# Four gated branch products: the gates' read-back issued after the recurrence, products in place, the last branch summed block by block

## The chip, the cores and the metric

The kernel runs on one core of a Trainium2 chip. The metric is the device time of one launch in microseconds (us). The core has five engines that run their own instruction streams and meet at semaphores: TensorE (PE; its weight loads are PEld), VectorE (DVE), ScalarE (ACT), GpSimd (POOL) and SyncE (SP, which here only issues weight loads). A transfer is issued on a queue of SP or of POOL (SPq, POOLq) and lands later.

## The reference

The program is two layers of a "first block", followed by one "second block". In each layer of the first block a normed input `h` (256 tokens, width 1024) is projected; four mixers of width 256 (sparse attention, retention, the RWKV-7 recurrence, a short convolution) give one output each, and the branches are merged with gates, which are part of the same projection:

```
gate_m  = sigmoid(h @ w_in[:, gate columns of branch m])     m = 0..3, each 256 x 1024
merged  = sum over m of gate_m * (o_m @ w_branch[m])
x       = x + rms_norm(merged @ w_mix_out) * gain
```

The kernel writes sigmoid(z) as (tanh(z/2) + 1) / 2: the tanh is what is stored, a product is `(stored + 1) * (o_m @ w_branch[m])`, and the factor 1/2 is applied once when the sum is copied out. Cross attention with the memory `mem` and a feed-forward part follow, then the second block with its 32 experts.

## The kernel before, in words

Everything is kept transposed: channels on the 128 partitions, 256 tokens along a row. Matrix products are made from halves: each 1 MB unit of weights that SP loads into one of four ring slots is copied to a rounded high half by ScalarE (`upper`, a 128x2048 ACTIVATE of 1.9 us) and subtracted to a low half by VectorE (`lower_part`, a 128x2048 TENSOR_TENSOR of 2.3 us); TensorE then makes three matmuls for each product (`mm3`, line 583). The halves lie in three buffers. Each engine's program calls `unit()` once for each weight unit in the same order, and each call on ScalarE and VectorE splits as far as two units ahead (LOOK = 2). So the place of the `unit()` calls in each program sets where the splits stand in its queue. Call the four units of `w_branch` m0 to m3, and the first ones of `w_mix_out` m4 and m5: the call for m0 splits m2, and so on. SP may load into a slot when VectorE has made the low half of the unit that was in it (line 2710).

`fill_list` (line 142) names 27 projections of `h` that are strewn between the small dependent steps of the mixers, so that TensorE has work. The last 16 are the gates: for gate n, ScalarE writes the tanh into one of two staging buffers `stg` (line 1374), and GpSimd stores it to DRAM, `gate_d`, 256 KB each (`gates`, lines 2622 to 2629), because the on-chip memory is full of the recurrence's matrices. Gates 14 and 15 are made after `y_of(1)`, the recurrence's last step on TensorE (lines 890 to 894); between and behind them stand the mean and the variance of y (`ymean`, `yvar`), and there `mix end` is marked.

VectorE norms y (lines 2222 to 2235): subtract the mean, square (`ysq`), wait for ScalarE's root (`yvar`, line 1521), reciprocal, two products, scale and add, and gives the third branch's output `yout`; ScalarE copies its high half `oT2`, VectorE writes the low half.

GpSimd then waits for `mix end` on three engines and for all gate stores, and issues four read-backs of 1 MB into `L.Gt`, each 128 partitions by 2048 (lines 2662 to 2668), and the load of `mem` (line 2669). `L.Gt`, two buffers `L.mg` and `L.mt` of 2048 columns, and `L.mem` share the arena with the mixers' tiles.

TensorE makes the branch products in the order BRANCHES = (0, 1, 3, 2), four groups of 12 matmuls for each branch, each group into a PSUM bank (lines 900 to 910). There are eight banks in turn, so group 9 waits for VectorE to have emptied the bank of group 1. VectorE's loop (lines 2239 to 2250) makes, for each branch, `unit()`, a wait for that branch's read-back, and four products, each of 128x512 and each waiting for the one before (the wait in `stt`, line 1880): branch 0 into `mg`, the others into `mt`. GpSimd adds `mt` to `mg` for branches 1 and 3 (lines 2670 to 2675), slice by slice; for branches 3 and 2 the product waits until `mt`'s slice was added. VectorE adds the last branch itself, four slices in a row (lines 2251 to 2254), ScalarE copies each slice's high half into `hTv[0]` (`merged`, line 1532), and VectorE writes the four low halves (lines 2255 to 2258). With the last of them `tok_out` starts on TensorE (lines 911, 912).

The functions concerned, `pool`, `scalar` and `vector`, are called once for each engine:

Of the kernel before, what the change touches and what calls it, by code (L numbers as in the profile page):

```python
# [262 lines left out]
def build(nc, W, CW, CS, CO, PR, PR2, GB, x_in, mem_in, out, scratch, bias_d, gate_d):  # L263
    ctx = ExitStack()
    with ctx:
# [1003 lines left out]
        def scalar(ac, branch):  # L1269
# [70 lines left out]
            for l in range(2):  # L1340
# [178 lines left out]
                fill()  # L1519
                ac.wait_ge(s_dve, V["ysq", l])  # L1520
# [6 lines left out]
                for m in range(4):  # L1527
                    unit()
                for jj in range(4):
                    js = slice(2 * jj, 2 * jj + 2)  # L1530
                    ac.wait_ge(s_dve, V["sum", jj, l])
                    act(hTv[0][:, js, :], L.mg[:, js, :], ACT.Copy, "merged", jj, l, scale=0.5)
# [334 lines left out]
        def vector(ve, branch):  # L1867
# [99 lines left out]
            for l in range(2):  # L1967
# [257 lines left out]
                tt(L.t2, L.t1, L.t1, MUL, "ysq", l)  # L2225
                ve.wait_ge(s_act, A["yvar", l])
# [5 lines left out]
                tt(L.t1, L.t1, L.gg, MUL, "yout", l)  # L2232
                ve.wait_ge(s_act, A["oT2", l])
                lower(oT[2], L.t1, "oT", 2, l)
                V.mark("mix end", l)
                ve.wait_ge(s_pe, P["mix end", l])


                for n, m in enumerate(BRANCHES):
                    unit()  # L2240
                    ve.wait_ge(s_gin[m], 16 * (l + 1))
                    for jj in range(4):
                        gsl = L.Gt[:, 8 * m + 2 * jj:8 * m + 2 * jj + 2, :]
                        js = slice(2 * jj, 2 * jj + 2)
                        dst = L.mt if m else L.mg
                        ve.wait_ge(s_pe, P["merge", m, jj, l])
                        if n >= 2:
                            ve.wait_ge(s_pool, G["sum", BRANCHES[n - 1], jj, l])
                        stt(dst[:, js, :], gsl, 1.0, half(banks["merge", m, jj, l]), ADD, MUL, "merge", m, jj, l)
                        gone("merge", m, jj, l)  # L2250
                for jj in range(4):
                    js = slice(2 * jj, 2 * jj + 2)
                    ve.wait_ge(s_pool, G["sum", BRANCHES[2], jj, l])
                    tt(L.mg[:, js, :], L.mg[:, js, :], L.mt[:, js, :], ADD, "sum", jj, l)
                for jj in range(4):
                    js = slice(2 * jj, 2 * jj + 2)
                    ve.wait_ge(s_act, A["merged", jj, l])
                    stt(hTv[1][:, js, :], L.mg[:, js, :], 0.5, hTv[0][:, js, :].bitcast(F32), MUL, SUB, "merged", l)
# [355 lines left out]
        def pool(gp, branch):  # L2614
# [7 lines left out]
            def gates(l):  # L2622
                for n in range(16):
# [5 lines left out]
                    gp.dma_start(gate_d[:, 512 * g:512 * g + 512], flat(layers[l].stg[n % 2])).then_inc(s_gate[n % 2], 16)  # L2629

# [9 lines left out]
            for l in range(2):  # L2640
# [20 lines left out]
                gates(l)  # L2661
# [3 lines left out]
                for i in range(2):  # L2665
                    gp.wait_ge(s_gate[i], 16 * 8 * (l + 1))
                for m in range(4):
                    gp.dma_start(flat(L.Gt[:, 8 * m:8 * m + 8, :]), gate_d[:, 2048 * m:2048 * m + 2048]).then_inc(s_gin[m], 16)
                gp.dma_start(L.mem, mem_in.rearrange("b (t p) d -> p (b t) d", t=2)).then_inc(s_mem, 16)
                for m in BRANCHES[1:3]:  # L2670
                    for jj in range(4):
# [3 lines left out]
                        gp.tensor_tensor(L.mg[:, js, :], L.mg[:, js, :], L.mt[:, js, :], ADD).then_inc(s_pool, G("sum", m, jj, l))  # L2675
# [248 lines left out]
```

## Time and profile before

| | us |
|---|---|
| median of 3 runs (lowest to highest) | 2218.91 (2217.14 to 2219.31) |
| the profiled execution's own time | 2216.08 |
| its span in the trace | 2214.3 |
| TensorE busy | 1954.1 (88%) |
| VectorE busy | 1441.0 (65%) |
| ScalarE busy | 1145.8 (52%) |
| GpSimd busy | 70.0 (3%) |

In the trace, lines such as L202 or L212 are those of the small helpers of `Seq` (188 matmul, 198 activation, 202 tensor_tensor, 209 tensor_scalar with two operations, 212 scalar_tensor_tensor, 225 reciprocal, 231 dma_start), so the tiles and the time tell which step it is. "arena" and "rounded" are the working memory, "ring" the loaded weights, "hl" their halves, "ax" the mixers' outputs, "ht" the split input of the next product. A bracket at the end of a timeline line is the engine's idle time before it and who ended it. All microseconds inside the trace count from the span's start.

### The profile page before, as it was taken

Reading aid. Unit: us, or ns where it says so; the run is one execution under the profiler, and the core shown is the slowest. Engines: PE = TensorE matmul, PEld = TensorE weight load, DVE = VectorE, ACT = ScalarE, POOL = GpSimd, SP = SyncE. Lnnn points to the kernel's source line nnn. Section 1 sums busy time; section 2 is a strip of 40 time slices with the busy share of each in tenths; the row PEclk is TensorE's granted clock in tenths of the full one; section 3 lists DMA queues with packets and bytes.
Section 4 is the critical chain, followed back from the end, with each engine's and each line's share of the span. In section 5 each row is a group of like instructions: output and inputs, shape, how many; then the busy total and the mean of one; then the engine's idle time right before and its main releaser. Section 6 shows DMA issues by size and latency. Waiting matters only on the chain.

```text
span 2214.3 us, 30326 instructions
## 1 busy us (share of the span) xinstructions
PE 1954.1 (88%) x13010; PEld 1784.8 (81%) x13010; DVE 1441.0 (65%) x1379; ACT 1145.8 (52%) x1194; POOL 70.0 (3%) x94
## 2 busy tenths in 40 slices
PE   4988996897999788999699799797759999999997
PEld 3978996887998778998688798697657888888885
DVE  3677646535555567745643655665659989999996
ACT  2533333444444443233443444455349888888884
POOL 0000003000000000002100000000000000000000
PEclk9999998998999889999899999998869999999999
DMA  6333345433555333346443445331329989999994
GB/s 257 125 123 115 120 167 218 163 134 115 190 184 179 129 133 114 125 143 232 148 154 126 162 182 192 141 137 70 121 106 357 369 354 365 365 374 376 360 364 179
DMA packets 64523, 440.86 MB, mean 199 GB/s; under 512 B 7372, under 2 KB 7372, under 8 KB 14592
## 3 DMA queue, kind: packets, MB, share of 16 engines
q1 hardware_dynamic: 55296, 399.63, 48.2%
q0 software_dynamic: 8096, 35.30, 4.2%
q10 hardware_dynamic: 992, 3.93, 0.4%
q8 instruction: 104, 1.70, 0.3%
q14 instruction: 35, 0.29, 0.0%
HBM read 428.61 MB, written 10.23 MB: 198 GB/s over the span
## 4 chain that ended last, share of the span: by engine, by line
PE 67%; DVE 18%; ACT 10%; DMA 2%; issue 2%; POOL 1%; DVEq 0%; ACTq 0%; POOLq 0%
PE psum L188 65%; ACT hl L198 4%; DVE ring_low L202 3%; DVE arena L212 3%; DVE ht L202 2%; PE psum L192 2%; DVE hl L202 2%; DVE rounded L212 2%; DVE rounded L202 2%; DVE arena L202 2%; ACT arena L198 2%; POOL arena L202 1%; ACT gn L198 1%; ACT rounded L198 1%; DVE arena L225 1%
## 5 line engine op out<-in xcount | busy, mean ns | idle before, releaser
L202 DVE TENSOR_TENSOR hl<-ring,hl 128x2048 fp32r<-128x2048 f32 (+1 forms) x190 | 430.7, 2268 | 386.7 <-ACT hl L198 386.6
L188 PE MATMUL psum<-ht,hl 128*128 128x256 f32 x4992 | 625.8, 287 | 15.4 <-DVE hl L202 9.8
L198 ACT ACTIVATE hl<-ring 128x2048 fp32r<-128x2048 f32 (+1 forms) x286 | 536.3, 1895 | 193.0 <-PE psum L188 167.4
L188 PEld LDWEIGHTS psum<-ht,hl 128*128 128x128 f32 x4992 | 611.6, 194 | 26.2 <-DVE hl L202 10.3
L198 ACT ACTIVATE arena<-psum 128x512 f32<-128x512 f32 (+7 forms) x242 | 123.4, 510 | 498.4 <-PE psum L188 475.3
L188 PE MATMUL psum<-hl,ax 128*128 128x512 f32 (+1 forms) x1608 | 356.1, 358 | 6.1 <-DVE ax L202 5.0
L188 PEld LDWEIGHTS psum<-hl,ax 128*128 128x128 f32 x1608 | 267.9, 194 | 47.4 <-DVE ax L202 5.3
L202 DVE TENSOR_TENSOR ring_low<-ring,hl 128x2048 fp32r<-128x2048 f32 x96 | 215.3, 2285 | 21.6 <-ACT hl L198 21.6
L188 PE MATMUL psum<-arena 128*128 128x128 f32 (+6 forms) x1520 | 198.7, 300 | 33.7 <-ACT arena L198 23.6
L188 PEld LDWEIGHTS psum<-arena 128*128 128x128 f32 (+2 forms) x1520 | 181.8, 185 | 46.3 <-ACT arena L198 25.3
L188 PE MATMUL psum<-hl,ht 128*128 128x256 f32 (+1 forms) x1056 | 132.9, 288 | 30.3 <-DVE ht L212 27.5
L188 PEld LDWEIGHTS psum<-hl,ht 128*128 128x128 f32 x1056 | 130.6, 197 | 32.5 <-DVE ht L212 27.9
L188 PE MATMUL psum<-rounded 128*128 128x512 f32 (+1 forms) x576 | 123.6, 352 | 9.2 <-DVE rounded L202 3.6
L192 PE MATMUL psum<-cst,arena 128*128 128x128 f32 x286 | 51.1, 347 | 88.4 <-DVE arena L212 64.4
L202 DVE TENSOR_TENSOR arena<-arena 128x512 f32<-128x512 f32 (+8 forms) x148 | 90.3, 610 | 59.1 <-ACT arena L198 43.0
L192 PEld LDWEIGHTS psum<-cst,arena 128*128 128x128 f32 x286 | 44.2, 182 | 94.9 <-DVE arena L212 42.0
L202 DVE TENSOR_TENSOR rounded<-arena,hl 128x2048 fp32r<-128x2048 f32 x48 | 107.7, 2285 | 18.2 <-ACT hl L198 18.2
L188 PE MATMUL psum<-ax,hl 128*128 128x256 f32 x768 | 102.5, 299 | 14.9 <-DVE arena L212 14.9
L188 PEld LDWEIGHTS psum<-ax,hl 128*128 128x128 f32 x768 | 100.7, 207 | 16.6 <-DVE arena L212 15.6
L188 PEld LDWEIGHTS psum<-rounded 128*128 128x128 f32 x576 | 93.6, 196 | 23.9 <-issue 3.7
L202 DVE TENSOR_TENSOR ht<-ht_raw,hl 128x2048 fp32r<-128x2048 f32 x46 | 103.2, 2285 | 3.8 <-ACT hl L198 3.8
L188 PE MATMUL psum<-hl,rounded 128*128 128x512 f32 x256 | 104.1, 406 | 0.0
(116 smaller groups left out, 2026.8 us busy)
## 6 DMA issues: line engine op xcount, KB each, us to landing
ring<-W SPq DMA_DIRECT2D x284, 1024.0 KB, 5.0
arena<-W SPq DMA_DIRECT2D x48, 1024.0 KB, 7.9
ht_raw<-W SPq DMA_DIRECT2D x46, 1024.0 KB, 7.4
gate_d<-arena POOLq DMA_DIRECT2D x32, 256.0 KB, 3.8
arena<-gate_d POOLq DMA_DIRECT2D x8, 1024.0 KB, 9.8
gn<-GB POOLq DMA_DIRECT2D x10, 512.0 KB, 4.0
arena<-GB POOLq DMA_DIRECT2D x6, 512.0 KB, 5.1
ring<-W SPq DMA_DIRECT2D x4, 512.0 KB, 3.2
```

The source lines that it names most:

```text
L188: return Nothing() if self.e is None else self.e.matmul(o, a, b, start=start, stop=stop, skip_group_check=skip_group_check)
L192: return Nothing() if self.e is None else self.e.transpose(o, a, ident)
L198: return self.e.activation(o, a, f, bias=bias, scale=scale)
L202: return Nothing() if self.e is None else self.e.tensor_tensor(o, a, b, op)
L212: return Nothing() if self.e is None else self.e.scalar_tensor_tensor(out=o, in0=a, scalar=s, in1=b, op0=op0, op1=op1)
L225: return Nothing() if self.e is None else self.e.reciprocal(o, a)
```

## The change

GpSimd issues the read-backs of branches 0, 1 and 3 as soon as `y_of(1)` has left TensorE and ahead of the stores of gates 14 and 15, and that of branch 2 behind them. ScalarE's and VectorE's `unit()` calls move: the first stands before the root and behind `ysq`. VectorE makes branch 0's products before it waits for the root, two of branch 1's before the low half of `oT2` and two behind it. The products are written in place over the gates in `L.Gt`, so that no product waits for an add, and they no longer wait for VectorE's previous instruction. GpSimd adds into branch 0's part of `L.Gt`. For branch 2, VectorE goes slice by slice: product, sum, and the low half of the slice before. TensorE's program is unchanged.

```diff
@@ scalar @@
                 fill()
                 fill()
+                unit()
                 ac.wait_ge(s_dve, V["ysq", l])
                 root(L.yrb, "eps64", 1.0 / 64, "yvar", l)
...
-                for m in range(4):
+                for m in range(3):
                     unit()
                 for jj in range(4):
                     js = slice(2 * jj, 2 * jj + 2)
                     ac.wait_ge(s_dve, V["sum", jj, l])
-                    act(hTv[0][:, js, :], L.mg[:, js, :], ACT.Copy, "merged", jj, l, scale=0.5)
+                    act(hTv[0][:, js, :], L.Gt[:, 8 * BRANCHES[0] + 2 * jj:8 * BRANCHES[0] + 2 * jj + 2, :], ACT.Copy, "merged", jj, l,
+                        scale=0.5)
@@ vector @@
                 tt(L.t2, L.t1, L.t1, MUL, "ysq", l)
+                first = L.Gt[:, 8 * BRANCHES[0]:8 * BRANCHES[0] + 8, :]
+
+                def merge(m, jj):
+
+                    gsl = L.Gt[:, 8 * m + 2 * jj:8 * m + 2 * jj + 2, :]
+                    ve.wait_ge(s_gin[m], 16 * (l + 1))
+                    ve.wait_ge(s_pe, P["merge", m, jj, l])
+                    stt(gsl, gsl, 1.0, half(banks["merge", m, jj, l]), ADD, MUL, "merge", m, jj, l, after=False)
+                    gone("merge", m, jj, l)
+
+                unit()
+                for jj in range(4):
+                    merge(BRANCHES[0], jj)
                 ve.wait_ge(s_act, A["yvar", l])
                 rec(L.yrb, L.yrb)
...
                 tt(L.t1, L.t1, L.gg, MUL, "yout", l)
+                for jj in range(2):
+                    merge(BRANCHES[1], jj)
                 ve.wait_ge(s_act, A["oT2", l])
                 lower(oT[2], L.t1, "oT", 2, l)
                 V.mark("mix end", l)
+                for jj in range(2, 4):
+                    merge(BRANCHES[1], jj)
                 ve.wait_ge(s_pe, P["mix end", l])
 
 
-                for n, m in enumerate(BRANCHES):
-                    unit()
-                    ve.wait_ge(s_gin[m], 16 * (l + 1))
-                    for jj in range(4):
...
-                        stt(dst[:, js, :], gsl, 1.0, half(banks["merge", m, jj, l]), ADD, MUL, "merge", m, jj, l)
-                        gone("merge", m, jj, l)
+                unit()
+                for jj in range(4):
+                    merge(BRANCHES[2], jj)
+                unit()
+                unit()
+
+                def low(jj):
+                    js = slice(2 * jj, 2 * jj + 2)
+                    ve.wait_ge(s_act, A["merged", jj, l])
+                    stt(hTv[1][:, js, :], first[:, js, :], 0.5, hTv[0][:, js, :].bitcast(F32), MUL, SUB, "merged", l, after=False)
+
                 for jj in range(4):
                     js = slice(2 * jj, 2 * jj + 2)
+                    merge(BRANCHES[3], jj)
                     ve.wait_ge(s_pool, G["sum", BRANCHES[2], jj, l])
-                    tt(L.mg[:, js, :], L.mg[:, js, :], L.mt[:, js, :], ADD, "sum", jj, l)
...
+                    tt(first[:, js, :], first[:, js, :], L.Gt[:, 8 * BRANCHES[3] + 2 * jj:8 * BRANCHES[3] + 2 * jj + 2, :], ADD,
+                       "sum", jj, l)
+                    if jj:
+                        low(jj - 1)
+                low(3)
                 unit()
                 unit()
@@ pool @@
-                gates(l)
+                gates(l, *range(14))
+                gp.wait_ge(s_pe, P["y", 1, l])
+                for n in range(3):
+                    gates_back(l, n)
+                gates(l, 14, 15)
+                gates_back(l, 3)
                 gp.wait_ge(s_pe, P["mix end", l])
                 gp.wait_ge(s_act, A["oT2", l])
                 gp.wait_ge(s_dve, V["mix end", l])
...
                 gp.dma_start(L.mem, mem_in.rearrange("b (t p) d -> p (b t) d", t=2)).then_inc(s_mem, 16)
```

The new function on GpSimd waits until the stores of that branch and those before it have landed, and issues one read-back:

```
            def gates_back(l, n):
                m = BRANCHES[n]
                for i in range(2):
                    gp.wait_ge(s_gate[i], 16 * (8 * l + 2 * n + 2))
                gp.dma_start(flat(layers[l].Gt[:, 8 * m:8 * m + 8, :]), gate_d[:, 2048 * m:2048 * m + 2048]).then_inc(s_gin[m], 16)
```

GpSimd's loop of adds is the same but for its operands: `first[:, js, :]` plus the slice of branch m in `L.Gt`.

## Rows read from the trace of the kernel before

**Rows 1.** The page: busy time, and the chain that ended last by engine.

```profile
PE 1954.1 (88%) x13010; PEld 1784.8 (81%) x13010; DVE 1441.0 (65%) x1379; ACT 1145.8 (52%) x1194; POOL 70.0 (3%) x94
...
PE 67%; DVE 18%; ACT 10%; DMA 2%; issue 2%; POOL 1%; DVEq 0%; ACTq 0%; POOLq 0%
```

**Rows 2.** Chain of waits, 290 to 372 us: start, us, what.

```profile
289.99 44.35 PE psum L188 x364
...
334.79 5.14 DMA arena<-gate_d
```

**Rows 3.** Timeline of the merge groups on TensorE: start, us, engine, line, operation.

```profile
323.69 12.07 PE L188 MATMUL psum<-ax,hl 128*128 128x256 f32 x96
...
340.79 13.89 PE L188 MATMUL psum<-ax,hl 128*128 128x256 f32 x96 [5.02 <-DVE arena L212]
```

**Rows 4.** Timeline, the same stretch: products, sums, the next stage's start.

```profile
339.95 3.06 DVE L212 SCALAR_TENSOR_TENSOR arena<-arena,psum 128x512 f32<-128x512 f32 x4 [2.32 <-DMA arena<-gate_d]
...
342.33 0.69 DVE L212 SCALAR_TENSOR_TENSOR arena<-arena,psum 128x512 f32<-128x512 f32 x1
342.93 2.29 DVE L202 TENSOR_TENSOR hl<-ring,hl 128x2048 fp32r<-128x2048 f32 x1
...
346.13 15.00 POOL L202 TENSOR_TENSOR arena<-arena 128x512 f32<-128x512 f32 x8 [8.54 <-DVE arena L212]
...
368.04 13.95 PE L188 MATMUL psum<-hl,ht 128*128 128x256 f32 x96 [13.36 <-DVE ht L212]
...
378.33 1.06 ACT L199 ACTIVATE arena<-arena 128x1024 f32<-128x1024 f32 x1
```

**Rows 5.** Timeline of the second layer: TensorE's first matmuls of `tok_out`.

```profile
1065.67 9.54 PE L188 MATMUL psum<-hl,ht 128*128 128x256 f32 x64 [14.12 <-DVE ht L212]
```

**Rows 6.** Waits of SP's queue, 300 to 400 us: total, times, longest.

```profile
SPq L231 <- DVE hl L202: 87.0, 11, 15.7
```

**Rows 7.** Timeline, the recurrence's end: y(1), and the last gate's steps.

```profile
308.85 1.99 PE L188 MATMUL psum<-arena 128*128 128x128 f32 x20
...
317.31 1.91 ACT L198 ACTIVATE hl<-ring 128x2048 fp32r<-128x2048 f32 x1
...
323.43 0.60 ACT L198 ACTIVATE arena<-psum 128x512 f32<-128x512 f32 x1 [4.20 <-PE psum L188]
...
324.32 0.54 POOL L231 DMA_DIRECT2D gate_d<-arena  x1 [6.07 <-ACT arena L198]
```

**Rows 8.** DMA issues, 300 to 400 us: count, size, us to landing.

```profile
arena<-gate_d POOLq DMA_DIRECT2D x4, 1024.0 KB, 9.7
gate_d<-arena POOLq DMA_DIRECT2D x4, 256.0 KB, 3.4
arena<-mem POOLq DMA_DIRECT2D x1, 1024.0 KB, 18.0
```

**Rows 9.** Timeline: the norm of y, and the issue of `mem`.

```profile
325.62 0.69 ACT L198 ACTIVATE arena<-psum,cst 128x512 f32<-128x512 f32 x1
326.34 3.35 DVE L225 RECIPROCAL arena<-arena 128x512 f32<-128x512 f32 x1 [3.26 <-ACT arena L198]
...
332.81 0.63 ACT L198 ACTIVATE ax<-arena 128x512 fp32r<-128x512 f32 x1 [6.49 <-DVE arena L202]
...
335.35 2.29 DVE L202 TENSOR_TENSOR hl<-ring,hl 128x2048 fp32r<-128x2048 f32 x1 [1.18 <-ACT hl L198]
336.88 0.71 POOL L231 DMA_DIRECT2D arena<-mem  x1
```

**Rows 10.** Timeline of GpSimd: two of its eight sums, each by itself.

```profile
349.00 3.16 POOL L202 TENSOR_TENSOR arena<-arena 128x512 f32<-128x512 f32 x1
...
352.30 1.30 POOL L202 TENSOR_TENSOR arena<-arena 128x512 f32<-128x512 f32 x1
```

**Rows 11.** Stretches: busy us per engine, then PEclk, DMA share, GB/s.

```profile
344.70:345.70 1.00, 1.00 (x7) 1.00 (x6) 0.87 (x2) 0.00 (x0) 0.00 (x0) 0.50 0.98 418
373.00:374.00 1.00, 1.00 (x10) 1.00 (x10) 0.00 (x0) 0.00 (x0) 0.00 (x0) 1.00 0.97 410
```

More of the change, by code:

```diff
@@ L2235, in vector @@
                 V.mark("mix end", l)
+                for jj in range(2, 4):
+                    merge(BRANCHES[1], jj)
                 ve.wait_ge(s_pe, P["mix end", l])
-                for n, m in enumerate(BRANCHES):
-                    unit()
-                    ve.wait_ge(s_gin[m], 16 * (l + 1))
-                    for jj in range(4):
[L2243 to L2248, printed above, removed]
-                        stt(dst[:, js, :], gsl, 1.0, half(banks["merge", m, jj, l]), ADD, MUL, "merge", m, jj, l)
-                        gone("merge", m, jj, l)
+                unit()
[7 more added lines that the diff above has]
+                    stt(hTv[1][:, js, :], first[:, js, :], 0.5, hTv[0][:, js, :].bitcast(F32), MUL, SUB, "merged", l, after=False)
                 for jj in range(4):
                     js = slice(2 * jj, 2 * jj + 2)
+                    merge(BRANCHES[3], jj)
                     ve.wait_ge(s_pool, G["sum", BRANCHES[2], jj, l])
-                    tt(L.mg[:, js, :], L.mg[:, js, :], L.mt[:, js, :], ADD, "sum", jj, l)
[L2255 to L2258, printed above, removed]
+                    tt(first[:, js, :], first[:, js, :], L.Gt[:, 8 * BRANCHES[3] + 2 * jj:8 * BRANCHES[3] + 2 * jj + 2, :], ADD,
[3 more added lines that the diff above has]
+                low(3)
                 unit()
@@ L2620, in post, with gates @@
                 gp.dma_start(dst[:, 0:1024], GB[i:i + 1, :].broadcast_to([128, 1024])).then_inc(s_post, 16)
-            def gates(l):
-                for n in range(16):
+            def gates(l, *ns):
+                for n in ns:
                     g = 4 * BRANCHES[n // 4] + n % 4
@@ L2629, in gates @@
                     gp.dma_start(gate_d[:, 512 * g:512 * g + 512], flat(layers[l].stg[n % 2])).then_inc(s_gate[n % 2], 16)
+            def gates_back(l, n):
+                m = BRANCHES[n]
+                for i in range(2):
+                    gp.wait_ge(s_gate[i], 16 * (8 * l + 2 * n + 2))
+                gp.dma_start(flat(layers[l].Gt[:, 8 * m:8 * m + 8, :]), gate_d[:, 2048 * m:2048 * m + 2048]).then_inc(s_gin[m], 16)
             gp.wait_ge(s_const, 16)
@@ L2664, in pool @@
                 gp.wait_ge(s_dve, V["mix end", l])
[L2665 to L2668, printed above, removed]
                 gp.dma_start(L.mem, mem_in.rearrange("b (t p) d -> p (b t) d", t=2)).then_inc(s_mem, 16)
+                first = L.Gt[:, 8 * BRANCHES[0]:8 * BRANCHES[0] + 8, :]
                 for m in BRANCHES[1:3]:
@@ L2674, in pool @@
                         gp.wait_ge(s_pool, G.n)
-                        gp.tensor_tensor(L.mg[:, js, :], L.mg[:, js, :], L.mt[:, js, :], ADD).then_inc(s_pool, G("sum", m, jj, l))
+                        gp.tensor_tensor(first[:, js, :], first[:, js, :], L.Gt[:, 8 * m + 2 * jj:8 * m + 2 * jj + 2, :],
+                                         ADD).then_inc(s_pool, G("sum", m, jj, l))
                 gp.wait_ge(s_dve, V["mem", l, "xn", 1])
```

## The prediction

> **What bounds the kernel now.** The page comes first. TensorE is busy for 88% of the span and carries 67% of the chain that ended last; VectorE carries 18% [rows 1]. So a change on VectorE and the queues pays only where TensorE stands still for them. The change touches one stretch, which occurs twice (once per layer), so I read the chain of waits there: up to 334.3 us it is TensorE all the way, then comes 5.14 us of the gates' read-back, and after that the chain runs over GpSimd and VectorE until TensorE resumes [rows 2]. The timeline shows the two holes in TensorE. The first eight merge groups (branches 0 and 1, 96 matmuls) end at 335.8; the ninth needs a PSUM bank that the first product has not yet emptied, and starts at 340.79. The last 96 end near 354.7, and `tok_out` starts at 368.04, when the last `merged` is written [rows 3, 4]. The second hole, 13.36 us, sets the end. The first one moves it only in so far as products, sums and the split into high and low halves finish earlier. The second layer repeats it 697.6 us later [rows 5]. Weight loads are not the limit: the queue of SP itself waits for VectorE's split of the old slot, 87 us in this window [rows 6].
>
> **Part 1: the read-back moves forward.** Before, it is issued at 334.79, after `mix end`, and the first product runs at 339.95 [rows 2, 4]. After, GpSimd issues three of the four (3 MB) once y(1) is done, near 310.9 [rows 7]. The four of before land in a median of 9.7 us, and the transfer behind them, the fifth, in 18.0 us [rows 8]. I expect the three by 316 to 325, since one weight load also falls in between. Branch 0's is first in the queue and needed at 328.2 (part 2). The stores of gates 14 and 15 (the last is issued at 324.32 and takes 0.54, [rows 7]) now queue behind these three; ScalarE waits for neither store, because no gate 16 follows. The fourth read-back waits for both stores: 324.32 plus the store's 3.4 us [rows 8] is 327.7, plus 5 to 10 us gives 333 to 338; its first use is after 351. So its cost is nothing, covered by 13 us. The load of `mem`, the next on that queue, is no longer behind 4 MB; ScalarE reads it ten microseconds after `tok_out` starts (378.33, [rows 4]), so it neither costs nor gives.
>
> **Part 2: the first four products go ahead of the norm.** ScalarE now makes the high half of one more weight unit (m2) before the root. Gate 15's tanh starts at 323.43; with some 0.5 us for it and 1.91 for the high half, that one ends at 325.8 [rows 7]. The root, at 325.62 before (0.69), ends by 325.62 + 1.91 + 0.69 = 328.2 [rows 9], while VectorE is busy anyway. VectorE's low half of m2, which stood at 335.35 behind the norm, runs from 325.9 to 328.2. Four products follow. TensorE makes their groups of 12 matmuls at 1.5 us each (96 in 12.07 from 323.69, [rows 3]), so they leave it from 325.2 on, so only the last may be waited for, and hardly. With the wait for the previous one they were 0.80 us apart; an instruction without that wait followed after 0.60 (342.33 to 342.93) [rows 4]. The change drops the wait, so I take 0.60 to 0.80: 2.4 to 3.2 us, giving 330.6 to 331.4. The norm from the reciprocal to ScalarE's copy of `oT2` took 332.81 - 326.34 = 6.47 us [rows 7, 9], so `yout` is at 337.1 to 337.9, some 4.7 us later than before. Queued behind that: the oT2 halves and branch 2's merge groups on TensorE. TensorE has branch 3's groups until 341.8, as their banks are free now, so it is not kept waiting before that.
>
> **Part 3: the rest of the stretch.** Two products, the low half of `oT2` (0.7) and two products take 3.1 to 3.9 us: 340.2 to 341.8. Then comes the low half of m3 (2.29). Before, the third half began at 348.33, right behind these eight products and both halves; now they are done by 343 to 345. GpSimd's sums start after its `mem` issue (0.71, [rows 9]), near 340.2 instead of 346.13. Four products of branch 3 (2.4 to 3.2) bring VectorE to 345.8 to 348, and the halves of m4 and m5, now back to back, to 350.7 to 353.
>
> What can give this back is the meeting of VectorE and GpSimd. A GpSimd sum takes 1.30 us, but 3.16 where it meets VectorE's subtraction over 2048 columns (at 349.00, behind the half at 348.33) [rows 10]. So eight sums at a pitch of 1.43 are 11.5 us, and each meeting adds 1.86; before there were two (15.0 in all, [rows 4]). After, m3, m4 and m5 are met (5.6 us), and three or four of the short sums and `merged` steps of VectorE, which before all ran after GpSimd was done and now stand between its adds: 0.5 to 1.1 us each, I take 2 in all. 340.2 + 11.5 + 5.6 + 2 = 359.3 for the last add, against 361.1. The Trainium skill (SBUF — State Buffer, section "SBUF: two separate sides") says that VectorE, with two SBUF inputs, and GpSimd take a shared port pair as an exclusive lock, and the loser waits for the whole instruction. The trace agrees, 3.16 us beside 1.30; by a shared bandwidth instead of a lock the short meetings would cost next to nothing and the sum would be some 2 us a layer better.
>
> Behind GpSimd's last add before came one product, four sums and four `merged`: from 346.13 + 15.00 = 361.1 to 368.04, 6.9 us. After, behind that add come sum 2, `merged` 1, the last product, sum 3, ScalarE's high half beside `merged` 2, and `merged` 3: six steps of 0.6 to 0.75, some 4.1 us. The high half of slice 3 and the low one of slice 2 run side by side. That gives 363.4 by the round numbers; walking both queues in step, with the 0.60 pitch, I get 362.0, and with the 0.72 pitch 363.0 to 363.7. I take **362.6**, since most operands stand ready early and the 0.60 row is the same kind of neighbour: 5.4 us earlier than 368.04, per layer.
>
> **The bounds.** Best: every pitch 0.60 and GpSimd's adds slipping between for free: 361.3, a gain of 6.7. Worst: pitch 0.80, four short meetings at 1.1 and all three long ones: 340.6 + 11.5 + 5.6 + 4.4 + 4.3 = 366.4, a gain of 1.6. TensorE's clock does not change this: after the first hole the granted clock still stands at 0.50 (1.2 GHz) at 345.7, 5 us after the restart; after the long one it is 1.00 (2.4 GHz) in the stretch from 373 us [rows 11]. In the changed kernel it starts at half again, and `tok_out`'s first 96 matmuls take 13.95 us [rows 4]. The hole stays at some 12 to 13 us, so this stays. If TensorE still pauses for m3 (341.8 to 343.5), branch 2 ends by 350 at full clock, 352.6 at half; VectorE reaches it at 351. That costs at most a microsecond, inside the bounds.
>
> **The sum.** 2 x 5.4 = 10.8 us off the profiled execution's 2216.08 us (span 2214.3): 2205.3. The median of the runs shown, 2218.91, is 2.8 above that execution, so the forecast is **2208.1 us**, with 2204.5 to 2211.5 as this case's own range.
>
> **The rivals.**
> *The port gives it back* (18%). Each short step loses its turn and GpSimd's adds stay what ends the stretch. For: eight short VectorE steps now stand among four of its adds, and two 2048-column subtractions stand back to back, where an add may lose twice running. Against: with five microseconds of lead, that takes four lost turns. Gain 1.6 to 3 us a layer: 2213 to 2215.7.
> *The start of the gates' read-back has lost its cover* (6%, slower). The first product now stands in front of the norm, so if branch 0's megabyte lands late, the norm, oT2, branch 2 and everything behind wait. It decides at 328.2 us, 17 us after issue, and costs more than it gives from 333.6 on. For: a transfer in this queue did take 18.0 us, behind four others, and 3 MB now meet weight loads. Against: this one is first, and the first before took 5.1. Landing at 336, it would cost 2.4 net a layer: 2223.7 us.
> *The time is not passed on* (8%): `tok_out` or the norm of `mem` is held by a weight unit or by the load of `mem`, so the earlier `merged` moves only a wait. Against: `mem` and both units are there well before. 2217 to 2219.
>
> **How the numbers follow.** A measurement of this kernel tells some 0.2% (4.4 us) from no change: the border is 2214.5. Forecast 68%, all faster. Of the port rival's 18%, two thirds are still faster. Faster 0.80; same 0.14 (6 of the port, 8 of not passed on); slower 0.06, the late read-back. The range 2204.5 to 2213.5 holds the forecast's own range and the near half of the port rival; the rest, under 20%, lies outside.
>
> **What would show it.** In the changed profile: no wait of VectorE for `gate_d` transfers; four products from 328.2 and the reciprocal near 331; no hole of 5 us after the first 96 merge matmuls, but a short one near 342; GpSimd's first add near 340 and more than two adds at about 3 us; `tok_out` near 362.6 and, in the second layer, near 1054.9 (5.4 from its own 1065.67 and 5.4 from the first). The forecast is wrong if VectorE idles before its first product, if `oT2` is later than 339, if GpSimd's last add ends past 361, or if `tok_out` starts within 2 us of its old place.

## The result and the profile after

The changed kernel took 2200.18 us (median of 4 runs, 2198.70 to 2201.41) against 2218.98 before (2217.14 to 2219.31): ratio 0.9914, interval 0.9902 to 0.9926. That is 18.8 us less where 10.8 were forecast, and below the forecast range. Timed again on two later occasions, the same kernel gave 2206.79 and 2202.97 us, 10.1 and 15.8 below the kernel before beside it. So the first question is what of the 18.8 us belongs to the change.

The page of the changed kernel, its busy times and the chain by engine; against [rows 1], TensorE is busy 8.3 us less with the same 13010 matmuls:

```profile
PE 1945.8 (89%) x13010; PEld 1777.6 (81%) x13010; DVE 1444.3 (66%) x1379; ACT 1146.1 (52%) x1194; POOL 76.4 (3%) x94
...
PE 67%; DVE 19%; ACT 10%; issue 1%; DMA 1%; POOL 1%; ACTq 0%; DVEq 0%; POOLq 0%
```

The timeline of the first layer's stretch in the changed kernel (start, us, engine, line, operation, count, idle before and who ended it). This execution is 0.6 us ahead of the one of before when the merge groups start (323.12 against 323.69, [rows 3]):

```profile
310.59 1.60 POOL L231 DMA_DIRECT2D arena<-gate_d  x3 [0.68 <-PE psum L188]
...
323.12 17.82 PE L188 MATMUL psum<-ax,hl 128*128 128x256 f32 x144
323.35 1.91 ACT L198 ACTIVATE hl<-ring 128x2048 fp32r<-128x2048 f32 x1
...
325.29 2.29 DVE L202 TENSOR_TENSOR hl<-ring,hl 128x2048 fp32r<-128x2048 f32 x1 [2.78 <-ACT hl L198]
...
327.50 2.66 DVE L212 SCALAR_TENSOR_TENSOR arena<-arena,psum 128x512 f32<-128x512 f32 x4
...
330.26 3.35 DVE L225 RECIPROCAL arena<-arena 128x512 f32<-128x512 f32 x1
...
336.73 0.63 ACT L198 ACTIVATE ax<-arena 128x512 fp32r<-128x512 f32 x1 [9.39 <-DVE arena L202]
...
339.80 3.77 DVE L202 TENSOR_TENSOR hl<-ring,hl 128x2048 fp32r<-128x2048 f32 x1
340.12 17.97 POOL L202 TENSOR_TENSOR arena<-arena 128x512 f32<-128x512 f32 x8
...
343.63 7.49 PE L188 MATMUL psum<-ax,hl 128*128 128x256 f32 x48 [2.68 <-DVE hl L202]
345.89 5.70 DVE L202 TENSOR_TENSOR hl<-ring,hl 128x2048 fp32r<-128x2048 f32 x2
...
355.20 1.75 DVE L212 SCALAR_TENSOR_TENSOR ht<-arena,ht 128x512 fp32r<-128x512 f32 x1
...
362.07 10.14 PE L188 MATMUL psum<-hl,ht 128*128 128x256 f32 x70 [10.96 <-DVE ht L212]
```

Here the forecast can be followed row by row. Nobody waits for a read-back. Twelve groups run through without a hole, where before there was one of 5.02 us after the eighth; a hole of 2.68 us stands in front of the last four groups, for the low half of m3. Two VectorE instructions show what they paid to GpSimd's adds: the half of m3 took 3.77 instead of 2.29 us, a `merged` step 1.75 instead of 0.69. `tok_out` starts at 362.07.

From the first merge matmul to `tok_out`'s first is what I call the stretch. It fell from 368.04 - 323.69 = 44.35 to 38.95 us in the first layer, and from 44.68 to 38.89 in the second: **11.2 us in all**. The forecast was 10.8. The second layer's stretch begins with this row before (it ends at 1065.67, [rows 5]),

```profile
1020.99 12.07 PE L188 MATMUL psum<-ax,hl 128*128 128x256 f32 x96
```

and begins and ends with these in the changed kernel:

```profile
1009.32 17.82 PE L188 MATMUL psum<-ax,hl 128*128 128x256 f32 x144
...
1048.21 13.23 PE L188 MATMUL psum<-hl,ht 128*128 128x256 f32 x96 [10.95 <-DVE ht L212]
```

But the second layer's `tok_out` starts at 1048.21, 17.5 us earlier than in [rows 5]. The stretches and the head start of 0.6 us make 11.8 of that; 5.7 us were gained where the code is the same in both kernels. This piece, from `tok_out` of layer 1 to the merge groups of layer 2, is 4402 matmuls long. Views by stretch (us, PE, PEld, DVE, ACT and POOL busy, granted clock, DMA share, GB/s), first the kernel before:

```profile
368.00:1020.90 652.90, 594.84 (x4402) 564.13 (x4403) 365.06 (x385) 275.87 (x349) 15.81 (x28) 0.94 0.41 147
```

and the changed kernel:

```profile
362.10:1009.30 647.20, 588.62 (x4403) 558.30 (x4404) 365.27 (x385) 277.05 (x350) 17.47 (x31) 0.96 0.43 152
```

The piece is 5.7 us shorter. VectorE and ScalarE are as busy as before, to 1.2 us; TensorE does the same matmuls in 6.2 us less, and its granted clock is 0.96 instead of 0.94. TensorE's idle time is what it was, 58.1 us before and 58.6 after, so no wait became shorter. So the rest of the gain in this profile is TensorE's own time, at a higher granted clock, in code that was not touched.

### The profile page after: what moved, and what is told of

Read it like the earlier page. It is cut to its first block, busy times and chain, and to the rows that moved or that the text cites. A ratio compares the mean times of both kernels' runs of the same rounds, so it can differ in the third digit from the quotient of the medians.

```text
span 2196.9 us, 30296 instructions
## 1 busy us (share of the span) xinstructions
PE 1945.8 (89%) x13010; PEld 1777.6 (81%) x13010; DVE 1444.3 (66%) x1379; ACT 1146.1 (52%) x1194; POOL 76.4 (3%) x94
## 4 chain that ended last, share of the span: by engine, by line
PE 67%; DVE 19%; ACT 10%; issue 1%; DMA 1%; POOL 1%; ACTq 0%; DVEq 0%; POOLq 0%
PE psum L188 65%; ACT hl L198 4%; DVE ring_low L202 3%; DVE arena L212 3%; DVE ht L202 2%; PE psum L192 2%; DVE hl L202 2%; DVE arena L202 2%; DVE rounded L212 2%; DVE rounded L202 2%; ACT arena L198 2%; DVE arena L225 1%; ACT gn L198 1%; POOL arena L202 1%; ACT rounded L198 1%
## 5 line engine op out<-in xcount | busy, mean ns | idle before, releaser
L188 PE MATMUL psum<-ht,hl 128*128 128x256 f32 x4992 | 621.2, 285 | 15.8 <-DVE hl L202 9.8
```

The source lines that it names most:

```text
L188: return Nothing() if self.e is None else self.e.matmul(o, a, b, start=start, stop=stop, skip_group_check=skip_group_check)
```

## The experiments

All times are medians; "before" is the kernel before, timed beside each group on the same chip. There were four groups, each on another chip (4, 11, 15 and 1). The stretches are taken from each kernel's profiled execution. Two theories stood against each other. **Queue theory**: the change saves what the stretch saves, and the 18.8 us would need a second effect of the change on the queues. **Clock theory**: the stretch gives 11 us; the rest is where TensorE's half-clock spells fall in the unchanged code.

### The parts of the change

The read-back alone, in the kernel before:

```diff
-                gates(l)
+                gates(l, *range(14))
+                gp.wait_ge(s_pe, P["y", 1, l])
+                for n in range(3):
+                    gates_back(l, n)
+                gates(l, 14, 15)
+                gates_back(l, 3)
...
-                for i in range(2):
-                    gp.wait_ge(s_gate[i], 16 * 8 * (l + 1))
-                for m in range(4):
-                    gp.dma_start(flat(L.Gt[:, 8 * m:8 * m + 8, :]), gate_d[:, 2048 * m:2048 * m + 2048]).then_inc(s_gin[m], 16)
```

> The kernel before with the early read-back alone. The stretch from TensorE's yvar sums to the start of tok_out is 43.8 us in the kernel before (324.3 to 368.0) and 38.4 in the changed one (323.7 to 362.1). Queue theory: the first product starts right behind the half of m2 (near 337.8 instead of 339.95), everything behind it moves by the same, 41.7 us per layer, and 4.3 us off the total. Clock theory: the same stretch, but the total differs from twice the stretch's gain by several us, because the half-clock spells of other stretches come out longer or shorter.

Measured: 2210.03 us, before 2218.01 (ratio 0.9961, 0.9947 to 0.9976). The stretches are 42.15 and 42.48, 4.4 us less in all, as expected; the total fell by 8.0. The timeline of this run:

```profile
334.88 2.29 DVE L202 TENSOR_TENSOR hl<-ring,hl 128x2048 fp32r<-128x2048 f32 x1 [1.18 <-ACT hl L198]
...
337.31 3.06 DVE L212 SCALAR_TENSOR_TENSOR arena<-arena,psum 128x512 f32<-128x512 f32 x4
...
338.14 13.23 PE L188 MATMUL psum<-ax,hl 128*128 128x256 f32 x96 [2.85 <-DVE arena L212]
```

The first product follows the half of m2 at once, 2.2 us earlier when counted from the first merge matmul (14.1 instead of 16.3 us behind it), and TensorE's hole falls from 5.02 to 2.85 us. So the early read-back alone is worth 2.2 us a layer.

The changed kernel with the norm ahead of all products (ScalarE's first `unit()` goes back behind the root as well):

```diff
-                unit()
-                for jj in range(4):
-                    merge(BRANCHES[0], jj)
                 ve.wait_ge(s_act, A["yvar", l])
...
-                for jj in range(2):
-                    merge(BRANCHES[1], jj)
                 ve.wait_ge(s_act, A["oT2", l])
...
-                for jj in range(2, 4):
-                    merge(BRANCHES[1], jj)
                 ve.wait_ge(s_pe, P["mix end", l])
+                unit()
+                for m in BRANCHES[:2]:
+                    for jj in range(4):
+                        merge(m, jj)
```

> The changed kernel, but with the norm of y ahead of all products (and the splits back in their old places). Queue theory: VectorE's eight first products end near 342.6 and the half of m3 near 345.5, some 2 us later than in the changed kernel: stretch 40.2 us, total 3.6 us above the changed kernel. Clock theory: stretch 40.2, total anywhere from 3 below to 10 us above the changed kernel.

Measured: 2209.40, before 2218.01 (0.9957, 0.9945 to 0.9969). The stretches are 39.80 each (40.2 expected), 0.9 us above the changed kernel's 38.9. Setting four products ahead of the norm and two ahead of the low half of `oT2` is worth 0.9 us a layer. The total lies 9.2 us above the first result of the changed kernel and 2.6 above its second.

The last branch as before, products, sums, low halves in rows:

```diff
+                for jj in range(4):
+                    merge(BRANCHES[3], jj)
                 for jj in range(4):
                     js = slice(2 * jj, 2 * jj + 2)
-                    merge(BRANCHES[3], jj)
                     ve.wait_ge(s_pool, G["sum", BRANCHES[2], jj, l])
                     tt(first[:, js, :], ...)
-                    if jj:
-                        low(jj - 1)
-                low(3)
+                for jj in range(4):
+                    low(jj)
```

> The changed kernel, but the last branch as before: four products, four sums, four low halves in a row. Queue theory: fewer meetings of VectorE with GpSimd's adds, but the low halves all stand at the end: stretch 38.4 plus or minus 0.7 us, total within 1.5 us of the changed kernel. Clock theory: the stretch the same, the total still off by up to several us.

Measured: 2199.88 (4 runs), before 2218.01 (0.9914, 0.9892 to 0.9936); that is 0.3 us from the first result of the changed kernel, where up to 1.5 was expected, and 6.9 below its second. The stretches are 38.25 and 38.17 (38.4 expected): 0.7 us a layer *shorter*. Summing block by block does not help. It lengthens GpSimd's adds, among which its short steps stand: the sixth add took 1.71 us, and 1.27 here. GpSimd's adds in this run:

```profile
338.83 17.46 POOL L202 TENSOR_TENSOR arena<-arena 128x512 f32<-128x512 f32 x8
...
357.56 2.49 DVE L212 SCALAR_TENSOR_TENSOR ht<-arena,ht 128x512 fp32r<-128x512 f32 x4
```

They take 17.46 instead of 17.97 us, and the four low halves behind them go through in 2.49, at 0.60 us each.

The wait for VectorE's own previous instruction kept in the products:

```diff
-                    stt(gsl, gsl, 1.0, half(banks["merge", m, jj, l]), ADD, MUL, "merge", m, jj, l, after=False)
+                    stt(gsl, gsl, 1.0, half(banks["merge", m, jj, l]), ADD, MUL, "merge", m, jj, l)
```

> The changed kernel, but each product waits again for VectorE's previous instruction. Queue theory: 16 products at 0.80 instead of 0.61 us, about half of it hidden behind waits for GpSimd: stretch 39.5 to 40.5 us, total 2 to 4 us above the changed kernel. Clock theory: the stretch the same, the total not twice that.

Measured: 2213.81, before 2218.01 (0.9977, 0.9965 to 0.9990). Stretches 41.50 and 41.06: 2.4 us a layer, above the 1 to 2 expected. The delays add up along VectorE's queue. Counted from the first merge matmul, `oT2` is 1.0 us later than in the changed kernel, the end of the low half of m3 1.4, the end of the halves of m4 and m5 2.8. Of that, 0.6 us come from these two halves, which fall otherwise against GpSimd's adds: 6.33 us instead of 5.70 for the two.

```profile
347.88 6.33 DVE L202 TENSOR_TENSOR hl<-ring,hl 128x2048 fp32r<-128x2048 f32 x2
```

With the read-back (2.2 us a layer) the removal of this wait is the largest part of the change. One part was never taken out by itself, the products written in place. The others add up to 2.2 + 0.9 + 2.4 - 0.7 = 4.8 of the 5.6 us a layer; the 0.8 that are left are its share or what the parts do to each other, and no run separates the two.

### Adding work to shift what follows

Three additions whose result is not used (2.2 us by their durations) ahead of the last low halves of layer 1, in the kernel before:

```diff
+                if l == 0:
+                    for _ in range(3):
+                        tt(L.mt[:, 0:2, :], L.mg[:, 0:2, :], L.mg[:, 0:2, :], ADD)
                 for jj in range(4):
                     js = slice(2 * jj, 2 * jj + 2)
                     ve.wait_ge(s_act, A["merged", jj, l])
```

> The kernel before with three more 128x512 additions on VectorE (0.73 us each) ahead of the last low halves of the first layer: tok_out of that layer starts 2.2 us later, nothing else is changed. Queue theory (a delay on the chain is paid one for one, and what follows takes the same time): total 2.2 us above the kernel before, and the piece from tok_out of layer 1 to the merge groups of layer 2, the same code in all kernels, stays at 653.0 us. Clock theory (what follows depends on where it falls against the changes of the granted clock): that piece falls to about 647 to 649, and the kernel with more work is the faster one, by 1 to 4 us in the median.

Measured: 2221.15, before 2219.74 (1.0008, 0.9992 to 1.0024). The first layer's stretch grew by 2.0 us. The piece behind the additions did fall, from 652.90 to 645.5 us:

```profile
369.50:1015.00 645.50, 587.57 (x4402) 557.85 (x4403) 365.10 (x385) 275.73 (x349) 15.83 (x28) 0.96 0.42 148
```

But the last piece, from layer 2's `tok_out` to TensorE's last matmuls some 9 us before the end of the span, rose to 1151.3 from the 1139.5 of the kernel before:

```profile
1065.70:2205.20 1139.50, 1034.25 (x6050) 911.14 (x6050) 820.62 (x682) 716.86 (x649) 4.25 (x8) 0.94 0.63 240
```

The shorter piece is what the clock theory said, the gain in the median is not: what one piece gained the other lost. Whether the additions shortened the piece or this launch did, one execution can't tell.

The same three additions in the changed kernel (ahead of `low(3)`, on `first`), and five of them:

```diff
+                if l == 0:
+                    for _ in range(3):
+                        tt(L.mt[:, 0:2, :], first[:, 0:2, :], first[:, 0:2, :], ADD)
                 low(3)
```

> The changed kernel with the same three additions ahead of the last low half of the first layer: tok_out 2.2 us later. Queue theory: total 2.2 us above the changed kernel, the piece behind it 647.3 us as there. Clock theory: the piece rises to 650 to 653 us and the total by 5 to 9 us.

> The changed kernel with five such additions: tok_out 3.6 us later. Queue theory: total 3.6 us above the changed kernel, so above the one with three. Clock theory: the piece behind tok_out is back at 647 to 648 us and the total 3 to 5 us above the changed kernel, so below the one with three additions although it does more.

Measured: 2213.28 (2204.12 to 2217.37) with three, 2213.40 with five, before 2219.74. The stretches grew by 2.0 and 3.5 us, the totals by 13 us against the first result of the changed kernel, and their means by 8.4 and 9.1 us against the mean of all its runs, which came later (2204.4). Not one for one, as queue theory has it; but the five came out no better than the three, so the forecast of the clock theory for the five missed. The middle pieces were 650.7 and 650.2, where 650 to 653 and 647 to 648 were expected. The first of these looks like a hit and is none: the unedited changed kernel had 650.5 as well when it was profiled again, in both further occasions below.

### Is it the kernel or the launch?

The changed kernel itself, unedited:

> The changed kernel itself once more. So far it has four runs, 2198.7 to 2201.4 us, while neighbours that differ from it by 2 to 4 us of delay lie at 2207 to 2213. If its place against the clock is a property of the kernel, it comes out at 2199 to 2202 again; if it was the launches, it spreads to 2205 and above as they do, and its median rises to 2203 to 2208.

Measured: 2206.79 (2200.59 to 2211.52), before 2216.86 (0.9946, 0.9926 to 0.9966). This is the decisive run. Its profiled execution has the same stretches, 38.94 and 38.87 us, and a span 12.8 us longer than the first one's (cores and granted clock, first the first profile of the changed kernel, then this one):

```profile
core 0: 2196.9 us, clock 0.944
```

```profile
core 0: 2209.7 us, clock 0.935
```

The piece behind layer 2's `tok_out` in the first profile of the changed kernel:

```profile
1048.20:2187.50 1139.30, 1033.91 (x6050) 911.17 (x6050) 820.93 (x682) 718.05 (x650) 4.27 (x8) 0.94 0.63 240
```

and in this one:

```profile
1051.40:2200.40 1149.00, 1043.23 (x6050) 918.67 (x6050) 821.58 (x683) 717.99 (x650) 4.26 (x8) 0.93 0.63 238
```

One program, the same 6050 matmuls, the same work on VectorE and ScalarE, and 9.7 us between the two executions; TensorE alone is 9.3 us busier, at a lower granted clock, and its idle time in the piece is the same to 0.4 us. The middle piece differs by another 3.3 us (650.5 against 647.2). The 9.7 us are not spread evenly. In ten slices of 100 us, from 100 us behind that `tok_out` on, the two executions agree within four matmuls in eight, and in two the longer one does 14 fewer (485 and 471 at clocks of 0.98 and 0.95; 506 and 492 at 0.98 and 0.97); the last eight matmuls take 3.67 instead of 2.13 us. Nor is it a matter of the chip: the six runs of this occasion were made on one chip and go from 2200.59 us at a mean clock of 0.942 to 2211.52 at 0.935.

Once more, to have three occasions:

> The changed kernel a third time. Its first four runs had a median of 2200.2 us, the next six 2206.8 (2200.6 to 2211.5), the kernel before 2217 to 2220. If the work alone is the change's, 10.8 us below the kernel before of the same chip: near 2207, with both kinds of runs in it (near 2201 and near 2211), and the profiled stretches again 38.9 us. If the first four were the rule, near 2200.

Measured: 2202.97 (2198.98 to 2211.67), before 2218.78 (0.9928, 0.9908 to 0.9949); stretches 38.94 and 38.87, clock 0.935. This profile (2211.67 us) repeats the second one (2211.52) on another chip almost to the digit: the middle piece took 650.56 and 650.54 us, and from layer 2's `tok_out` to the start of the last eight matmuls it was 1145.98 us in both, against 1137.52 in the first profile. Over the three occasions the changed kernel has 16 runs: eleven from 2198.7 to 2203.5 (mean clock 0.938 to 0.944) and five from 2210.6 to 2211.7 (0.935 or 0.936), with none between; median 2202.7 and mean 2204.4. The 79 runs of the kernel before that were made beside the experiments have a median of 2218.3 and a mean of 2218.9. The change is then worth 14.5 us in the mean, 11.2 of them in the stretches. If every run counts as independent, the interval of that mean is some 12.0 to 17.0 us.

### TensorE kept busy in the hole

Eighty matmuls into a free bank (their result is not used) between the last merge group and `tok_out`; a hundred in the kernel before:

```diff
+                spare = turn.now["turn"][0]
+                of, at = freed.get(turn.now["had"].get(spare), (V, 1))
+                pe.wait_ge(of.sem, at)
+                for _ in range(80):
+                    pe.matmul(psum[:, spare, 0:256], oT[2][0][:, 0, 0:128], oT[2][0][:, 0, :], True, True)
                 pe.wait_ge(s_dve, V["merged", l])
```

> The changed kernel with 80 idle matmuls (into a free bank, the result is not used) in TensorE's hole before tok_out, some 10 us of it, in both layers. Clock theory: TensorE's granted clock stays at 1.00 over the hole, tok_out's first 96 matmuls take 11.8 instead of 13.6 to 14 us and the stretch's length stays at 38.9; at least 3.6 us off the total, give or take the spells elsewhere. Queue theory alone: no change, as TensorE is not what the stretch waits for.

> The kernel before with 100 such matmuls in the same hole of both layers. Clock theory: 3.6 to 5 us off its total. Against the changed kernel with its holes filled, the difference by work alone is twice the stretch's gain, 10.8 us; more than 14 or less than 7 us would be spells elsewhere.

Measured: 2206.17 for the changed kernel filled, 2215.88 for the one before filled, before 2216.86. The changed kernel with its hole filled (timeline, then the two stretches in it):

```profile
351.35 9.76 PE L188 MATMUL psum<-ax 128*128 128x256 f32 x80
362.58 11.78 PE L188 MATMUL psum<-hl,ht 128*128 128x256 f32 x96 [1.47 <-DVE ht L212]
```

```profile
351.00:362.00 11.00, 10.11 (x85) 9.90 (x83) 9.50 (x13) 2.73 (x5) 7.16 (x4) 1.00 0.44 165
362.00:374.00 12.00, 11.42 (x95) 11.43 (x96) 5.95 (x5) 6.41 (x8) 0.00 (x0) 1.00 0.28 92
```

and without the filling:

```profile
351.00:362.00 11.00, 0.12 (x1) 0.00 (x0) 9.57 (x13) 3.23 (x5) 6.65 (x4) 0.69 0.37 144
362.00:374.00 12.00, 11.93 (x87) 11.93 (x88) 4.61 (x3) 5.26 (x6) 0.00 (x0) 0.85 0.26 89
```

The clock stays at 1.00 and `tok_out`'s first 96 matmuls take 12.1 us from start to start of the next, instead of 13.6 in the first and 14.7 in the second profile of the changed kernel. That part is shown. In the kernel before it worked in the first layer only: 12.1 instead of 14.3 us, and 13.6 instead of 13.7 in the second. The total did not follow: 0.6 us below the changed kernel of the same group, and 1.0 below for the kernel before, where 3.6 was the least expected. In both the last piece came out long (1149.1 and 1146.9 us, 1139.3 at best in the unfilled ones), so it seems to have been lost again elsewhere; that rests on one profiled execution of each. The two filled kernels differ by 9.7 us, their stretches by 11.2.

### A version that beats both

GpSimd's adds and VectorE's instructions with two inputs in SBUF lengthen each other: of the eight adds in the changed kernel three took 3.1 to 3.2 us, behind the halves of m3, m4 and m5, three 1.5 to 1.7 us among the short steps, and two 1.3 us. If they exclude each other, together they fill the time from 340 us to `tok_out`. The half of m5 is needed only by `tok_out`'s second unit, so it can stand behind the sum:

```diff
                     merge(BRANCHES[2], jj)
                 unit()
-                unit()
...
                 low(3)
+                unit()
                 unit()
                 unit()
```

> The changed kernel, but VectorE makes the low half of the sixth weight unit (m5) behind the last low half of the sum instead of ahead of the last branch. Port theory (from 340 us to tok_out VectorE's two-input work in SBUF, 12.3 us, and GpSimd's adds, 10.4 us, exclude each other and together fill the stretch): stretch 38.9 us falls by 2.3 to 3 us to about 36.3 per layer. Rival (the stretch is set by the chain of slices of the last branch alone): it falls by less than 1 us, as the half was hidden behind GpSimd's adds. The total follows by twice that, plus or minus what the clock does.

Measured: 2207.48, before 2219.74 (0.9943, 0.9926 to 0.9960); stretches 37.12 and 37.04, 1.8 us less each. GpSimd's adds in it:

```profile
340.14 16.14 POOL L202 TENSOR_TENSOR arena<-arena 128x512 f32<-128x512 f32 x8
345.91 2.41 DVE L202 TENSOR_TENSOR hl<-ring,hl 128x2048 fp32r<-128x2048 f32 x1
```

One long meeting less, 16.14 instead of 17.97 us, which is the 1.8 us of the stretch. That is more than the rival allowed (less than 1 us) and less than the port theory's 2.3 to 3: its cause is right and its size too large, for VectorE did not fill the time (it waited 2.02 us for GpSimd's adds at 350.9). By its total alone this version is not shown to be better than the changed kernel: it is 12.3 us below the kernel before, and the changed kernel was 18.8, 10.1 and 15.8. With the hole filled by 66 matmuls as well:

> The version with the low half of m5 behind the sum, with 66 such matmuls in the hole. Its stretches are 1.85 us shorter than the changed kernel's, so by work it is 3.7 us below the filled changed kernel; the clock may add or take some 5 us.

> The version with the half of m5 behind the sum and the filled holes once more. First time 2195.4 us (2191.7 to 2204.4), 21.5 below the kernel before. By work and the faster start of tok_out I expect 10.8 + 3.7 + 4.0 = 18.5 us below the kernel before, 2199; with the spread of the first time 15 to 22 us.

Measured: 2195.39 (before 2216.86, ratio 0.9911, 0.9889 to 0.9932) and 2199.74 (before 2218.78, 0.9913, 0.9891 to 0.9934). Over both, 12 runs have a mean of 2198.1 us, against 2204.4 of the changed kernel. This is the best version found: 21.5 and 19.0 us below the kernel before (18.5 expected for the second). The difference of 6.3 us from the changed kernel has an interval of some 4 us either way, and 3.5 of it are in the stretches. The first of the two lies 10.8 us below the filled changed kernel of its group, where 3.7 by work and up to 5 by the clock were expected.

### All of them together

What the stretches give (both layers, less 89.0 us of the kernel before) against what the total gave (less "before" of the same group):

| kernel | stretches, us | by them | measured | rest |
|---|---|---|---|---|
| changed, first | 77.8 | -11.2 | -18.8 | -7.6 |
| changed, second | 77.8 | -11.2 | -10.1 | +1.1 |
| changed, third | 77.8 | -11.2 | -15.8 | -4.6 |
| read-back alone | 84.6 | -4.4 | -8.0 | -3.6 |
| norm first | 79.6 | -9.4 | -8.6 | +0.8 |
| sums last | 76.4 | -12.6 | -18.1 | -5.5 |
| own wait kept | 82.6 | -6.5 | -4.2 | +2.3 |
| before, 3 additions | 90.7 | +1.7 | +1.4 | -0.3 |
| changed, 3 additions | 79.9 | -9.2 | -6.5 | +2.7 |
| changed, 5 additions | 81.3 | -7.7 | -6.3 | +1.4 |
| half of m5 behind | 74.2 | -14.9 | -12.3 | +2.6 |
| changed, filled | 78.1 | -10.9 | -10.7 | +0.2 |
| before, filled | 89.3 | +0.3 | -1.0 | -1.3 |
| half behind, filled, first | 74.3 | -14.7 | -21.5 | -6.8 |
| half behind, filled, second | 74.4 | -14.6 | -19.0 | -4.4 |

The rest has a mean of -1.5 us and goes from -7.6 to +2.7 (for the filled ones it also holds the faster start of `tok_out`). So what the stretches give and what the total gave go the same way, but for the filled kernel before, where both are near nothing. A total of four to eleven runs adds up to 7.6 us of its own, which is more than the interval of one comparison shows.

## Why the prediction was right and where it failed

**Part 1** held: the read-backs were issued at 310.59, nobody waited for one, the fourth and `mem` cost nothing.

**Part 2** held once the 0.6 us of this execution are taken off, the first product to 0.1 us and the others inside their ranges: first product 327.50 (forecast 328.2), reciprocal 330.26 (330.6 to 331.4), `oT2` 336.73 (337.1 to 337.9). The pitch without the wait was the 0.60 us that the one neighbour in [rows 4] had shown: the first three products started 0.60 and 0.59 us apart. The fourth started 0.79 behind the third, as its group left TensorE only then, so the four took 2.66.

**Part 3** held: GpSimd began at 340.12 (340.2) and took 17.97 us (19.1), the halves of m4 and m5 ended at 351.6 (350.7 to 353), `tok_out` at 362.07 (362.6). The three long meetings cost the 5.6 us of the sum; the short ones were over-sized, 1.05 us where the sum had 2. That the first layer's gain came out at 5.4 us to the digit is partly luck. Its own round numbers gave 363.4 for `tok_out`, the 362.6 came from walking the queues, and with the 0.6 us of this execution taken off GpSimd began half a microsecond late. In the second layer the gain was 5.8. The rule of the Trainium skill (SBUF — State Buffer, section "SBUF: two separate sides") that one of the two engines holds the shared port pair for its whole instruction and the other waits was borne out by the 3.77 and 1.75 us above and by the run with the half moved behind. The recorded starts do not show who is served first: the half of m3 is recorded from 339.80 and the add from 340.12, and yet the add took its 1.30 us and the half waited. I had read the rule as a risk; it was also the lever for the better version.

**The step that failed** is in the bounds: "TensorE's clock does not change this", and with it the silent term that all code outside the stretch takes the time that it took before. The bounds weighed the clock only inside the stretch and at `tok_out`'s first 96 matmuls, which were to take the 13.95 us of before and took 13.3 in the first profile and 14.4 in the second. In the changed kernel's first profile the middle piece took 647.2 instead of 652.9 us, so the term put at nothing was 5.7 us; in the first result's median, what the stretches do not explain is 18.8 - 11.2 = 7.6 us. In its second and third profile the last piece took 1149.0 instead of 1139.3. What the clock takes is a cost of the whole program that differs from launch to launch, and a single profile is one draw of it. The forecast added the gain to one such draw of the kernel before. The range of 2204.5 to 2213.5 had no term for it: its lower end lay 1 us below the best bound of the stretch (2218.9 - 2 x 6.7 = 2205.5). It held the second occasion (2206.8), not the first (2200.2) or the third (2203.0); that the second fell inside is no more than the share of long runs in it. The 0.2% that the prediction took as what one measurement can tell was too small for the same reason: the three medians of one kernel differ by 6.6 us.

The rivals: the port did not give it back, GpSimd's adds took 17.97 us where the sum had 19.1; the late read-back did not come; "not passed on" was wrong, as the second layer's merge groups began 11.7 us earlier, more than the first had won, and TensorE idled no longer in the piece between (58.1 and 58.6 us).

**What stays open.** What places a launch against the clock's spells, and whether the changed kernel is placed favourably more often than the kernel before: its mean gain (14.5 us) is 3.3 above its stretches', with a spread in the table of the same size. The launch is not all of it, either. The five runs of the version with the half of m5 behind (2204.81 to 2208.62) lie in the gap between the changed kernel's two groups of runs, so each kernel seems to have places of its own, and nothing here says which. Whether the additions shifted the pieces is not shown: only the kernel before had a shorter one with them, once. Of the clock theory's three forecasts for their totals none came true against the first result of the changed kernel, and one does against its mean (8.4 us, 5 to 9 expected).

## What to carry to other kernels

Sum a change on the stretch that it touches, from the waits and the instruction pitches; that sum was right to half a microsecond per layer. Then compare, in both profiles, a piece of code that was not touched: if it differs by microseconds at the same count of matmuls and the same busy time of the other engines, and its granted clock differs with it, that part is TensorE's clock and not the saving that was summed, and one occasion of timing does not settle it. Where VectorE and GpSimd both work from SBUF, look for VectorE work of two inputs that can be moved out of the time in which GpSimd is on the path.

## What was not expected of the hardware

Two executions of one program differed by 12.8 us in span (2196.9 and 2209.7), with the same stretches to 0.02 us and the same busy time of VectorE and ScalarE in the last piece within 0.7 us; TensorE's mean granted clock was 0.944 and 0.935. The 16 runs of that program fall into two groups, 2198.7 to 2203.5 and 2210.6 to 2211.7 us, and two of the long ones, profiled on two chips, agree within 0.02 us in both long pieces. Filling a hole with idle matmuls kept the clock at 1.00 and made the next 96 matmuls 1.5 to 2.6 us faster, and yet left the total of the changed kernel within 0.6 us of the unfilled one of the same group. In the execution with 2.0 us of work added ahead of it, the unchanged middle piece was 7.4 us shorter than in the kernel before, and the last one 11.8 us longer.
